# Out-projection weight sums of a hybrid encoder step: sixteen of twenty moved from GpSimd additions to accumulating DMAs

## What is computed

```python
xn = rms_norm(x, pre_g)
u = jnp.einsum('btd,de->bte', xn, w_in)                      # 1024 -> 5120
xr, gr, cv_v, cv_g, gc = jnp.split(u, 5 equal parts, axis=-1)
y_r = rg_lru(causal_dwconv(xr, width 4)) * silu(gr)          # recurrent group, 1024 wide
v = silu(layer_norm(causal_dwconv(cv_v * sigmoid(cv_g), width 31)))
y_c = (v @ cv_w2 + cv_b2) * silu(gc)                         # conformer group, 1024 wide
y = jnp.einsum('btm,md->btd', jnp.concatenate([y_r, y_c], -1), w_out)   # 2048 -> 1024
return x + rms_norm(y, post_g), and the new states
```

## Time and profile before

| | |
|---|---|
| median of 3 runs | 808.17 us (808.12 to 810.3) |
| the profiled execution | span 806.3 us from first to last instruction; it has no device time of its own beside the span, which is 1.9 us under the median |
| PE busy | 783.2 us, 97% |
| DVE busy | 665.5 us, 83% |
| ACT busy | 422.1 us, 52% |
| POOL busy | 384.9 us, 48% |
| 16 DMA engines | 32.5% of their time in the hardware queue, 0.6% in the software queue |

### The profile page before, as it was taken

The page is one execution under the profiler, slowest core; times in us unless marked ns, Lnnn a source line. Parts: engine busy times, 40 slices in busy tenths (PEclk is TensorE's granted clock), DMA queues, the critical chain, the costliest instruction groups (busy, mean ns, idle before and its releaser), DMA issues. The chain is left out here.

```text
span 806.3 us, 12690 instructions
## 1 busy us (share of the span) xinstructions
PE 783.2 (97%) x5158; PEld 763.0 (95%) x5158; DVE 665.5 (83%) x564; ACT 422.1 (52%) x657; POOL 384.9 (48%) x215
## 2 busy tenths in 40 slices
PE   5999999999999999999999999999999799999996
PEld 4899999999999999999999989999999799999995
DVE  5589999999998986986995988982438899799894
ACT  6522374474474365365366379953515244566652
POOL 4325347346546446456556744010036896389220
PEclk9999999999999999999999999999999999999998
DMA  8311211211211121121121120423279463554683
GB/s 269 96 54 37 70 53 53 80 52 53 73 59 52 58 73 52 53 79 52 53 79 52 53 80 27 134 71 116 80 240 279 142 171 107 157 157 132 187 262 139
DMA packets 111404, 82.37 MB, mean 102 GB/s; under 512 B 3179, under 2 KB 101483, under 8 KB 111362
## 3 DMA queue, kind: packets, MB, share of 16 engines
q1 hardware_dynamic: 110432, 80.68, 32.5%
q0 software_dynamic: 928, 1.12, 0.6%
q10 hardware_dynamic: 2, 0.00, 0.0%
HBM read 68.55 MB, written 13.25 MB: 101 GB/s over the span
## 5 line engine op out<-in xcount | busy, mean ns | idle before, releaser
L919 PE MATMUL ps<-act_hi,w_hi 128*128 128x352 f32 (+4 forms) x1384 | 445.1, 322 | 5.6 <-DVE w_lo L2067 4.2
L921 PE MATMUL ps<-act_hi,w_lo 128*128 128x352 f32 (+4 forms) x1384 | 438.6, 317 | 0.0
L920 PE MATMUL ps<-act_lo,w_hi 128*128 128x352 f32 (+3 forms) x1320 | 420.2, 318 | 0.0
L1870 DVE SCALAR_TENSOR_TENSOR ps<-cv_in,par_cv,ps 128x1086 f32<-128x1086 f32 x232 | 313.9, 1353 | 7.8
L919 PEld LDWEIGHTS ps<-act_hi,w_hi 128*128 128x128 f32 x1384 | 260.5, 188 | 12.7 <-issue 7.2
L921 PEld LDWEIGHTS ps<-act_hi,w_lo 128*128 128x128 f32 x1384 | 261.1, 189 | 0.0
L920 PEld LDWEIGHTS ps<-act_lo,w_hi 128*128 128x128 f32 x1320 | 248.1, 188 | 0.2
L721 POOL TENSOR_TENSOR w_lo<-wstage,w_hi 128x1024 fp32r<-128x1024 f32 x40 | 97.3, 2447 | 74.7 <-ACT w_hi L1272 74.6
L920 PE MATMUL ps<-act_hi,w_hi 128*128 128x264 f32 (+2 forms) x256 | 73.7, 288 | 0.0
L1272 ACT ACTIVATE w_hi<-wstage 128x1024 fp32r<-128x1024 f32 x47 | 48.6, 1052 | 22.4 <-PE ps L921 15.4
L919 PE MATMUL ps<-act_lo,w_hi 128*128 128x264 f32 x192 | 55.5, 289 | 0.0
(11 more groups left out here) (241 smaller groups left out, 1048.5 us busy)
## 6 DMA issues: line engine op xcount, KB each, us to landing
wstage<-in_w_in SPq DMA_DIRECT2D x40, 512.0 KB, 3.9
wstage<-in_w_out SPq DMA_DIRECT2D x20, 512.0 KB, 5.0
w_stage<-in_w_out SPq DMA_DIRECT2D x19, 512.0 KB, 5.0
stage<-in_w_out SPq DMA_DIRECT2D x9, 512.0 KB, 4.1
silu_spill<-silu_gc SPq DMA_DIRECT2D x8, 528.0 KB, 2.7
yr_spill<-y_rg SPq DMA_DIRECT2D x8, 528.0 KB, 2.8
silu_l<-silu_spill SPq DMA_DIRECT2D x8, 528.0 KB, 3.7
yr<-yr_spill SPq DMA_DIRECT2D x2, 2112.0 KB, 11.1
```

Source lines behind the costliest of these rows:

```text
L919: pe.matmul(out, wh, xh, start=start, stop=False)
L920: pe.matmul(out, wh, xl, start=False, stop=False)
L921: return pe.matmul(out, wl, xh, start=False, stop=stop)
L1870: STT(out=acc, in0=src, scalar=w, in1=acc, op0=ALU.mult, op1=ALU.add).then_inc(taps, 1)
```

## The change

In the steps whose table entry is `ALU.add` POOL no longer adds. It waits until SP has loaded the first block, and issues a DMA that reads the second block from memory and adds it to the first in SBUF (`accum_op=ALU.add`). ACT waits for that DMA's semaphore, `wo_summed` of the slot. Such a step takes one slot of the ring and not two, so SP loads 32 blocks where it loaded 48, and POOL issues the other 16. The signs of the table are turned so that only product 3 (steps 12 to 15) has a difference; those four stay additions on POOL. The signs of the results are put right in the additions of DVE (`add_product`) and in one copy of ACT, with as many instructions as before. POOL makes `weight_sum(s + 3)` in its loop where it made `weight_sum(s + 2)`.

```diff
--- before.py
+++ after.py
@@ -149,9 +149,9 @@
 
 
 
-PRODUCTS = [((0, 0), ALU.add, (0, 1)), ((0, 1), ALU.subtract, (1, 1)), ((1, 1), None, None),
-            ((0, 0), ALU.add, (1, 1)), ((1, 0), ALU.add, (1, 1)), ((0, 0), None, None),
-            ((1, 0), ALU.subtract, (0, 0))]
+PRODUCTS = [((0, 0), ALU.add, (0, 1)), ((0, 1), ALU.add, (1, 1)), ((1, 1), None, None),
+            ((0, 0), ALU.subtract, (1, 1)), ((1, 0), ALU.add, (1, 1)), ((0, 0), None, None),
+            ((1, 0), ALU.add, (0, 0))]
 HT = KT // 2
 STEPS = len(PRODUCTS) * HT
 TH = TO // 2
@@ -164,7 +164,7 @@
     FIRST_BLOCK.append(len(BLOCKS))
     _a, _op, _b = PRODUCTS[_s // HT]
     BLOCKS.append((_s, 0, _a))
-    if _op is not None:
+    if _op is ALU.subtract:
         BLOCKS.append((_s, 1, _b))
 
 
@@ -176,7 +176,13 @@
 
 def weight_sums(s):
 
-    return sum(PRODUCTS[u // HT][1] is not None for u in range(s + 1))
+    return sum(PRODUCTS[u // HT][1] is ALU.subtract for u in range(s + 1))
+
+
+def weight_adds(s):
+
+    i = FIRST_BLOCK[s]
+    return sum(PRODUCTS[u // HT][1] is ALU.add and FIRST_BLOCK[u] % N_STAGE == i % N_STAGE for u in range(s + 1))
 
 
 def copies(s):
@@ -461,6 +467,7 @@
 
         wo_loaded = [sem(f"wo_loaded{i}") for i in range(N_STAGE)]
         wo_added = sem("wo_added")
+        wo_summed = [sem(f"wo_summed{i}") for i in range(N_STAGE)]
         b_sum = sem("b_sum")
         b_sum_v = sem("b_sum_v")
         b_high = sem("b_high")
@@ -487,6 +494,11 @@
         w_in_v = w_in.rearrange("d (k p) e -> p (d k) e", p=P)
         w_pw_v = cv_w_pw2.rearrange("d (k p) e -> p (d k) e", p=P)
         w_out_v = w_out.rearrange("d (h k p) e -> p (d h k) e", h=2, p=P)
+
+        def w_out_block(s, m, h):
+            e = m * HT + s % HT
+            return w_out_v[:, (1 - h) * KT:(2 - h) * KT, e * P:(e + 1) * P]
+
         xp_v = x_prompt.rearrange("b t d -> (b t) d")
         xs_v = x_sample.rearrange("b t d -> (b t) d")
 
@@ -634,9 +646,7 @@
                         sp.wait_ge(wo_added, weight_sums(u))
                     else:
                         sp.wait_ge(late_los, LATE_OUT + u + 1)
-                e = m * HT + s % HT
-                sp.dma_start(OUT_STAGE[i % N_STAGE], w_out_v[:, (1 - h) * KT:(2 - h) * KT, e * P:(e + 1) * P])\
-                    .then_inc(wo_loaded[i % N_STAGE], 16)
+                sp.dma_start(OUT_STAGE[i % N_STAGE], w_out_block(s, m, h)).then_inc(wo_loaded[i % N_STAGE], 16)
 
             def load_silu(h):
                 sp.wait_ge(yc, 4 + h + 1)
@@ -859,8 +869,12 @@
 
             def weight_sum(s):
 
-                i, op = FIRST_BLOCK[s], PRODUCTS[s // HT][1]
-                if op is not None:
+                i, (_, op, second) = FIRST_BLOCK[s], PRODUCTS[s // HT]
+                if op is ALU.add:
+                    pool.wait_ge(wo_loaded[i % N_STAGE], 16 * (i // N_STAGE + 1))
+                    pool.dma_start(OUT_STAGE[i % N_STAGE], w_out_block(s, *second), accum_op=op)\
+                        .then_inc(wo_summed[i % N_STAGE], 16)
+                elif op is ALU.subtract:
                     for b in (i, i + 1):
                         pool.wait_ge(wo_loaded[b % N_STAGE], 16 * (b // N_STAGE + 1))
                     TT(OUT_STAGE[i % N_STAGE], OUT_STAGE[i % N_STAGE], OUT_STAGE[(i + 1) % N_STAGE], op)\
@@ -902,8 +916,8 @@
                 pool.dma_start(dst, state_rows[row:row + n, :]).then_inc(st_out, 16)
             weight_sum(1)
             for s in range(-1, STEPS - 2):
-                if s >= 0:
-                    weight_sum(s + 2)
+                if s < STEPS - 3:
+                    weight_sum(s + 3)
                 for p in SUMMED:
                     n, k = (4 if p == 1 else 2), s - SUMS_FROM[p]
                     if 0 <= k < KT // n:
@@ -1659,8 +1673,11 @@
             def out_high(s):
 
                 i = FIRST_BLOCK[s]
-                if PRODUCTS[s // HT][1] is None:
+                op = PRODUCTS[s // HT][1]
+                if op is None:
                     act.wait_ge(wo_loaded[i % N_STAGE], 16 * (i // N_STAGE + 1))
+                elif op is ALU.add:
+                    act.wait_ge(wo_summed[i % N_STAGE], 16 * weight_adds(s))
                 else:
                     act.wait_ge(wo_added, weight_sums(s))
                 if s < 2:
@@ -1735,7 +1752,7 @@
                     act.wait_ge(b_low, 2 * KT)
                     A(two(c_half(HT + ei, 0)), got, ACT.Copy).then_inc(c_copied, 1)
                 elif p == 3:
-                    A(two(c_half(HT + ei, 1)), got, ACT.Copy).then_inc(c_copied, 1)
+                    A(two(c_half(HT + ei, 1)), got, ACT.Copy, scale=-1.0).then_inc(c_copied, 1)
                 if s >= FINAL:
                     f, e, h = s - FINAL, ei + (p in (4, 6)) * HT, p // 5
                     if p == 3:
@@ -2087,7 +2104,8 @@
                     TT(two(c_half(ei, 0)), got, two(c_half(ei, 1)), ALU.subtract).then_inc(c_added, 1)
                 elif p in (2, 3):
                     dve.wait_ge(c_added, additions(s - HT))
-                    TT(two(c_half(ei, 0)), two(c_half(ei, 0)), got, ALU.add).then_inc(c_added, 1)
+                    TT(two(c_half(ei, 0)), two(c_half(ei, 0)), got, ALU.subtract if p == 2 else ALU.add)\
+                        .then_inc(c_added, 1)
                 elif p == 4:
                     dve.wait_ge(c_copied, copies(s))
                     TT(two(c_half(lower, 0)), two(c_half(lower, 0)), got, ALU.add).then_inc(c_added, 1)
@@ -2095,7 +2113,7 @@
                 elif p == 5:
                     dve.wait_ge(c_added, additions(s - HT))
                     TT(two(c_half(ei, 1)), two(c_half(ei, 1)), got, ALU.add).then_inc(c_added, 1)
-                    TT(two(c_half(lower, 1)), two(c_half(lower, 1)), got, ALU.add).then_inc(c_added, 1)
+                    TT(two(c_half(lower, 1)), two(c_half(lower, 1)), got, ALU.subtract).then_inc(c_added, 1)
                 elif p == 6:
                     dve.wait_ge(c_added, additions(s - HT))
                     TT(two(c_half(lower, 1)), two(c_half(lower, 1)), got, ALU.add).then_inc(c_added, 1)
```

## The result

The changed kernel takes 831.92 us (830.15 to 833.01), the kernel before 808.2 us in the same series: ratio 1.0289, interval 1.0275 to 1.0303, +23.7 us. I had forecast 809.0 us within 804 to 814. The profiled execution of the changed kernel has a span of 829.2 us, 22.9 more than that of before.

A forecast was written before the change was run, and what follows sets the result against it. PE was taken as the bound, busy 783.2 of 806.3 us, with about 5.7 us in reach near 625 us. Terms +1.1 + 0.4 - 0.7 = +0.8 gave span 807.1, plus 1.9 to the median: 809.0 us, range 804.0 to 814.0.

The forecast's parts named there:

- They read and write no tile on POOL's own lanes, so DVE gets gaps instead of 2.4 us blocks.: On POOL: sixteen DMA issues of 0.95 us each replace additions of about 2.6 us and leave DVE free between.
- the alternation: POOL and DVE take turns, whichever comes second standing until the other's instruction ends; 7.2 us of it gone between 617.6 and 636.9.
- all three rivals: Read not delayed, 804.1 us (0.26); read later still, 811.7 us (0.29); landings too slow, some 818 us (0.05).
- Later: -0.7: From 700 us on, fewer weight sums crowd DVE and ACT's scaled rows come in time, saving 0.7 of 0.9 us.
- +1.1 and 0.4: Around steps 2 and 3: step 3 begins 1.1 us later, at 638.0, and 0.4 us more for the slow clock.
- L = 622.2: Landing of the last read of y_r, moved from 614.6 by 2.0 and 5.6 us.
- (b): Accumulations of steps 1 and 2 share the DMA engines with the read of y_r: 2 x 2.8 = 5.6 us of delay.
- rival 1: Software queue's transfers do not delay the read, by gaps or read served first; landing 615 to 617, 804.1 us; chance 0.26.
- is 613.9. No loss.: Step 1's accumulated sum lands at 613.9 us, in time for w_hi at 613.98.
- Rival 3: Landings of 12 us or more make ACT wait in each first step; 1 us in ten steps, some 818 us; chance 0.05.
- 2.8 with an end of 3.7: Time one accumulating DMA costs the sixteen DMA engines, in us; middle between a copy's 1.84 and double that, 3.7.
- +0.8: Net change forecast for the whole kernel: +1.1 + 0.4 - 0.7 us, a wash; chance 0.40.

The follow-up runs named there:

- Experiment 1: Changed kernel, but each of POOL's operand sums first waits for the end of the one before it: 811.62 us, ratio 1.0038.
- experiment 2: Changed kernel with plain copies in place of the sixteen accumulating DMAs: 823.76 us, ratio 1.0198.
- experiment 7: Kernel before plus three 1024-piece plain DMAs: ahead of the ten sums 809.99 us, with waits between sums 809.03, behind the sums 808.58, ahead into a spare tile 811.34.
- experiment 8: Kernel before plus one large plain DMA between first and second of the ten sums: to memory 821.08 us, to a spare tile (second kernel) 822.02 us.
- experiment 9: Changed kernel with step 19's sum alone made by a POOL addition again, the other fifteen by DMA: 816.25 us, ratio 1.0081.
- the gap: Each POOL operand sum waits for the end of the one before it; put into the changed kernel: 811.62 us.
- experiment 5: Changed kernel with accumulating DMAs for products 4 and 6 only, first eight sums by POOL: 822.88 us; with waits between operand sums 809.32 us.
- experiments 4 and 6: 4: changed kernel, step 1's DMA right behind step 0's, 833.13 us, with the gap 811.52. 6: changed kernel with the gap, step 1's sum by POOL, 813.1 us.

## Why the prediction was wrong

**The step that failed: "They read and write no tile on POOL's own lanes, so DVE gets gaps instead of 2.4 us blocks."** I carried the alternation over from the kernel before, where every row bears it out. With a DMA issue between POOL's sums it no longer held. A DVE instruction that started in the issue was overtaken by all of POOL's following sums. Experiment 1 shows it by taking POOL's unbroken run away, 2 shows that accumulation is not needed, 7 that the same traffic ahead of the ten sums does not do it by itself, and 8 makes it with one DMA, in its second kernel with one that moves 24 KB. Nothing in my sum or in my rivals had it; all three rivals were about transfers.

**"Later: -0.7".** It was +14. The row of ten sums that the kernel before issues without a pause was harmless only because DVE got its turn between them. I named its cover nowhere. This is 14 of the 23 us: 15.7 by experiment 9 taken away, 12.7 by experiment 8 put in, 13.6 by the gap in experiment 5.

**The first steps, +1.1 and 0.4.** They were +8.5. The 7.23 us w_lo accounts for 6.0 of it. The rest is a sum that landed late: w_lo of step 1 could start only at 620.14, so that even at 1.21 us it would have been ready at 621.35, 2.2 us after PE asked for it at 619.2.

**L = 622.2.** It was 616.7. The sum of 5.6 us for (b) let the read wait for all that two accumulations take. The read went ahead of the accumulations, as rival 1 said of it, and rival 1's reason was right while its time of 804.1 us was not. The Trainium skill ("DMA: Bandwidth & Descriptors", Issuing engines are not separate DMA queues) says that all DMAs interleave on the same 16 engines. The trace agrees: the read was delayed (2.1 us) and so were POOL's transfers (12.5 and 16.7 us to land, 6.1 at best). But most of the delay fell on POOL's, and my sum had put all of it on the read.

**Step 1's sum "is 613.9. No loss."** It landed at 619.0. Where two queues compete I had let the one win that mattered to me less. The paragraph "Later" says that a landing above 12 us makes every step pay: three of sixteen were above that (12.5, 16.7 and later a 12.8), and ACT waited for one of them, 4.8 us. Rival 3 had this wait in ten steps, at 818 us; it came in one.

**The prices.** The packets of an accumulation took 4.2 us of the sixteen engines' time where I took 2.8 with an end of 3.7, and a plain copy 1.8 as I had it. The ratio is 2.3. The Trainium skill ("Collectives: The Full Stack", the section on the bandwidth ceiling) gives 1.93 as the measured ratio of its copying to its adding collective; the trace has more for this DMA. As packets overlapped (share 1.31 and 1.41), 4.2 us is not time that the others lose, and so was the wrong price for the delay of the read. The row of an issue is 1.56 us long where I took 0.95, which a plain one does take (0.90).

**What of it the mechanism leaves over.** With the alternation restored (experiment 1) the change still costs some 3.5 us, and all of it lies at the first place: by the same pairing of matmuls, counted from 613 us on, it grows by 3.9 us at step 1 and stands at 4.4 at 700, and by the end it is 4.0. That is what came of the case for which I had forecast +0.8, though it holds what the gap itself costs. No run has the gap alone; with three DMAs that nobody waits for (experiment 7) it was 0.7 us over the kernel before. Moving it to another step (experiments 4 and 6) did not lessen it, and leaving the first eight sums to POOL did (809.32 us, 0.0012 over the kernel before). I take it for the accumulations that land late at a time when the engines are full, which is argued from where it falls and not shown by a run of its own.

**What I said would show it.** Of the signs of being wrong in kind, the last one fitted, "or if other stages than this one differ": the largest wait is 100 us away from the place that I had studied. No version beat the kernel before. The best, eight sums by DMA with the gap, is the same as it within what can be told.

## What to carry to other kernels

When a change puts a DMA issue into a run of GpSimd instructions, look at every unbroken run behind it, and at what VectorE has in flight at that moment. That both engines took turns in the trace before is no proof that they will. If they don't, one semaphore wait between the GpSimd instructions gives VectorE its turn back, here for 20 us. And look for a new wait in all places where the touched engine works, not only where the old wait was.

## What the runs showed of the hardware

- A VectorE instruction on two tiles that starts while GpSimd issues a DMA with additions behind it can be held until GpSimd's unbroken run ends: 4 to 7 us behind short runs, 12 to 14 us behind nine or ten sums, with GpSimd's sums starting 1.07 to 1.29 us apart. In ordinary runs of the same sums both get on (2.0 us a sum, DVE at its own pace). What in the chip does this stays open. So does why it missed a few cases: with three or four DMAs in a row ahead of the ten sums an instruction that started within one of the later issues got through after 1.21 us, in all three such kernels without the gap, and in the kernel with plain copies a w_lo did (637.81 us, 1.21 us long).
- The next sum appears 0.94 us after an accumulating issue begins, and its own row is longer by the rest, so a POOL row behind an issue must not be read as a slow sum.
- The packets of an accumulation of 512 KB from memory into a tile took 4.2 us of all sixteen DMA engines, those of a copy 1.8. With both queues at work these times overlap: the share reached 1.41. The least time to land was 6.1 us against 4.0 for the copy of experiment 2, and with a full hardware queue beside it an accumulation took up to 16.7 us, while that queue's own read was delayed 2.1.
- The clock after PE stood still: granted 0.50, the lower level of 1.2 GHz, in the window from 625 to 630 us behind 8.0 us of standing, and a mean of 0.74 from 740 to 750 behind 11.6. At both places it fell while PE still stood: 0.73 from 620 to 625 us with PE at 0.00, and 0.75 from 730 to 740 with PE busy for 0.29 us. In the kernel before it fell at 629.6 (0.81 from 629 to 630), 0.6 us after PE had resumed at 629.05, and not 0.9 as I had read it. The lower clock behind 600 us is 4.0 of the 5.6 us by which PE's busy time grew.
